# First mixer of a two-block network: the pooled half moved ahead of the heads and its projection between their halves

## What is computed

```python
def mixer_ab(x, norm, w_in, conv_w, conv_b, w_gx, b_gx, w_ga, b_ga, lam, w_pool, b_pool, pool_scale, w_out):
    z = rms_norm(x, norm) @ w_in
    z_gate = z[..., :W_A]
    z_rec = z[..., W_A:2 * W_A]
    z_pool = z[..., 2 * W_A:]
    xr = causal_dwconv(z_rec, conv_w, conv_b)
    y_a = jax.nn.gelu(z_gate) * rg_lru(xr, w_gx, b_gx, w_ga, b_ga, lam)
    y_b = multi_scale_pool(z_pool, w_pool, b_pool, pool_scale)
    return jnp.concatenate([y_a, y_b], axis=-1) @ w_out
```

## Time and profile before

| | |
|---|---|
| median of 3 runs | 3119.04 us (3116.56 to 3124.23) |
| the profiled execution | 3123.22 us |
| its span, first to last instruction | 3121.9 us |
| mean granted TensorE clock | 0.929 |

### The profile page before, as it was taken

How to read it: one execution, slowest core, us unless ns; L and a number is a source line. 1 busy time by engine, 2 the same in 40 slices (tenths; PEclk the granted TensorE clock), 3 DMA queues, 4 the chain that set the end, 5 groups by cost and what they waited for, 6 DMA issues and landing times. The chain is left out here.

```text
span 3121.9 us, 43004 instructions
## 1 busy us (share of the span) xinstructions
PE 2727.5 (87%) x18210; PEld 2154.1 (69%) x18210; DVE 1839.9 (59%) x2229; ACT 1216.8 (39%) x1553; POOL 279.5 (9%) x204
## 2 busy tenths in 40 slices
PE   6659999999999799999999798867869759399996
PEld 5437878888866378788887586645657647388885
DVE  5565545454568664454554665265565645399997
ACT  4434333232343342332323332233333212388884
POOL 1002000000000020100000100021120101123231
PEclk9879999999999899999999898979879889599998
DMA  4112322222211033222222342311110042499996
GB/s 149 51 45 92 121 81 95 95 95 95 101 60 49 23 106 107 81 95 95 95 95 95 108 155 98 121 34 24 24 32 15 6 152 85 185 374 378 383 369 235
DMA packets 88430, 366.74 MB, mean 117 GB/s; under 512 B 26032, under 2 KB 30256, under 8 KB 54320
## 3 DMA queue, kind: packets, MB, share of 16 engines
q1 hardware_dynamic: 78192, 339.33, 30.6%
q0 software_dynamic: 10048, 24.66, 2.3%
HBM read 346.62 MB, written 39.35 MB: 124 GB/s over the span
## 5 line engine op out<-in xcount | busy, mean ns | idle before, releaser
L471 PE MATMUL bank<-xg_hi,w_hi 128*128 128x512 f32 x1504 | 602.1, 400 | 11.9 <-DVE xg_lo L493 11.9
L471 PE MATMUL bank<-xg_lo,w_hi 128*128 128x512 f32 x1504 | 588.9, 392 | 0.0
L471 PE MATMUL bank<-xg_hi,w_lo 128*128 128x512 f32 x1504 | 588.8, 392 | 0.0
L458 DVE TENSOR_TENSOR w_lo<-w_raw,w_hi 128x2048 fp32r<-128x2048 f32 x165 | 378.0, 2292 | 218.3 <-ACT w_hi L454 217.9
L454 ACT ACTIVATE w_hi<-w_raw 128x2048 fp32r<-128x2048 f32 x165 | 314.2, 1905 | 275.6 <-PE bank L471 239.1
L471 PEld LDWEIGHTS bank<-xg_hi,w_hi 128*128 128x128 f32 x1504 | 285.3, 190 | 77.9 <-DVE w_lo L458 11.9
L471 PEld LDWEIGHTS bank<-xg_lo,w_hi 128*128 128x128 f32 x1504 | 285.0, 189 | 66.0 <-issue 7.5
L471 PEld LDWEIGHTS bank<-xg_hi,w_lo 128*128 128x128 f32 x1504 | 284.4, 189 | 60.2
L2771 DVE TENSOR_TENSOR w_lo<-e_w_raw,w_hi 128x2048 fp32r<-128x2048 f32 x77 | 174.5, 2285 | 11.2 <-ACT w_hi L2593 11.2
L2593 ACT ACTIVATE w_hi<-e_w_raw 128x2048 fp32r<-128x2048 f32 x77 | 147.7, 1918 | 29.9 <-PE bank L471 29.9
L609 DVE TENSOR_TENSOR x<-bank,x 128x512 f32<-128x512 f32 x88 | 60.5, 688 | 161.3 <-PE bank L471 161.3
(11 more groups left out here) (460 smaller groups left out, 5337.8 us busy)
## 6 DMA issues: line engine op xcount, KB each, us to landing
w_raw<-stream SPq DMA_DIRECT2D x165, 1024.0 KB, 4.9
e_w_raw<-expert_rows SPq DMA_DIRECT2D x63, 1024.0 KB, 9.6
w_raw<-expert_rows SPq DMA_DIRECT2D x33, 1024.0 KB
y_rows<-e_y_row SPq DMA_DIRECT2D x39, 512.0 KB
p_spill<-p_stage SPq DMA_DIRECT2D x36, 256.0 KB, 2.0
mix_gate<-p_spill SPq DMA_DIRECT2D x16, 256.0 KB, 4.6
na_bias<-bias_na SPq DMA_DIRECT2D x16, 224.0 KB, 4.6
rw_rkv<-p_spill SPq DMA_DIRECT2D x12, 256.0 KB, 6.4
```

The costliest lines, as they stand in the source:

```text
L458: V.tensor_tensor(ring(m)["lo"][m % SLOTS][:, :], ring(m)["raw"][m % RAW][:, :], ring(m)["hi"][m % SLOTS][:, :].bitcast(F32), ALU.subtract ...
L471: return T.matmul(out_ap, lhsT, rhs, start=first, stop=last, skip_group_check=True)
```

## The change

Five things change in the first mixer, and one at the start.

- The plan puts the pooled units first, then heads 0 to 4, then the two units of `ab_out_b`, then heads 5 to 7, then `ab_out_a`.
- A buffer `ab_under_y` lies in the same memory as `ab_y_hi` and `ab_y_lo`: the pooled groups' inputs and windows and all eight multipliers are kept there, each under the tile of y that is written later. The convolution's buffers are free all the time.
- TensorE projects the pooled groups first, does the group matmuls between heads 1, 2 and 3, and projects y's pooled half into tiles `xb` behind gates 3. Each other engine's order follows; ScalarE and VectorE run the first half's chain beside that, and VectorE adds the tiles `xb` to x between the outputs of heads 0 to 3.
- Behind the last gates TensorE opens six tiles `xa` with heads 0 to 3 (72 matmuls), and adds heads 4 to 7 when they are there.
- The norm tiles and the memory tiles now both run under `xa`, and GpSimd sums both in turns.
- At the start unit 1 is split before the squares and the reciprocal.

```diff
-    plan = [("ab_in", h) for h in range(8)] + [("pool_in", i) for i in range(2)]
-    plan += [("ab_out_a", i) for i in range(4)] + [("ab_out_b", i) for i in range(2)]
+    plan = [("pool_in", i) for i in range(2)] + [("ab_in", h) for h in range(5)]
+    plan += [("ab_out_b", i) for i in range(2)] + [("ab_in", h) for h in range(5, 8)]
+    plan += [("ab_out_a", i) for i in range(4)]
...
+        with ExitStack() as inner:
+            ab_under_y = sb(inner, "ab_under_y", [P, 2, KT, S])
...
+        act_split(A, 1)
...
+        dve_split(V, 1)
...
+    pool_u = [ab_under_y[:, 0, 4 + g, :] for g in range(4)]
+    pool_scratch = [[ab_under_y[:, 1, 4 + g, :], ab_tmp[g % 2][:, :]] for g in range(4)]
+    ab_mult = [ab_under_y[:, 1, h, :] for h in range(8)]
...
+        def open_out():
+            for j in range(ab_open):
+                n = units_of("ab_out_a", 4)[j // 2]
+                hi, lo = unit(n, 2 * P)
+                T.wait_ge(*w_lo.at(n))
+                cols = slice((j % 2) * P, (j % 2 + 1) * P)
+                b = take_bank(T, ("xa", j), dve_ab, "xa", j)
+                for k in range(4):
+                    T.wait_ge(*dve_ab.at("y_lo", k))
+                    split_matmul(T, b[:, :], hi[:, k, cols], lo[:, k, cols], ab_y_hi[:, k, :], ab_y_lo[:, k, :],
+                                 k == 0, False)
...
+        project_head(0)
+        project_head(1)
+        gates(0)
+        groups(0, 1)
+        project_head(2)
+        gates(1)
+        groups(2, 3)
+        project_head(3)
+        gates(2)
+        project_head(4)
+        gates(3)
+        pe_out(T, units_of("ab_out_b", 2), S, (ab_y_hi, ab_y_lo), range(4, 8), pe_ab, ("xb",),
+               ready=lambda k: dve_ab.at("yb_lo", k - 4))
+        project_head(5)
+        gates(4)
+        project_head(6)
+        gates(5)
+        project_head(7)
+        gates(6)
+        gates(7)
+        open_out()
+        pe_out(T, units_of("ab_out_a", 4), 2 * P, (ab_y_hi, ab_y_lo), range(KT), pe_ab, ("xa",), 1,
+               ready=lambda k: dve_ab.at("y_lo", k), opened={j: range(4, KT) for j in range(ab_open)},
+               after=lambda T: pe_xa_begin(T, 0))
...
-        for u in range(4):
-            pool_xa_mem(G, 0, u)
-        for i in range(1, 4):
+        pool_norm_sums(G, 1, lambda G, u: pool_xa_mem(G, 0, u))
+        for i in range(2, 4):
             pool_norm_sums(G, i)
```

More of the change, by code:

```diff
@@ L585, in pe_out, with act_out @@
             pe_norm_sums(T, i)
-    def act_out(A, units, cols, added, tag, i, xg_free, square_free, beside=None, after=None):
+    def act_out(A, units, cols, added, tag, i, xg_free, square_free, beside=None, after=None, taken=0):
         for u, n in enumerate(units):
-            act_take(A, n)
+            if u >= taken:
+                act_take(A, n)
             if beside:
@@ L598, in act_out, with dve_out @@
         act_norm_root(A, i)
-    def dve_out(V, units, cols, done, added, tag, i=None, bias=None, beside=None, after=None):
+    def dve_out(V, units, cols, done, added, tag, i=None, bias=None, beside=None, after=None, taken=0):
         for u, n in enumerate(units):
-            dve_take(V, n)
+            if u >= taken:
+                dve_take(V, n)
             if beside:
@@ new lines, in groups @@
+        def groups(*gs):
+            T.wait_ge(*group_load.at("w"))
+            for g in gs:
+                T.wait_ge(*dve_ab.at("pooled", g))
+                b = take_bank(T, ("group", g), dve_ab, "grouped", g)
+                matmul(T, b[:, :], ab_pool_w[:, g, :], pool_scratch[g][0]).then_inc(*pe_ab.mark("group", g))
+        def open_out():
[9 more added lines that the diff above has]
+                                 k == 0, False)
@@ L713, in pe_mixer @@
         for g in range(4):
             b = take_bank(T, ("pool", g), dve_ab, "u", g)
[L715 to L722, removed]
@@ L723, in pe_mixer @@
-        pe_out(T, units_of("ab_out_b", 2), S, (ab_y_hi, ab_y_lo), range(4), pe_ab, ("xb",), 1,
-               ready=lambda g: dve_ab.at("yb_lo", g), after=lambda T: pe_xa_begin(T, 0))
+            project(T, place[("pool_in", g // 2)], 2 * P, g % 2, ring1["xg"], range(KT), b, pe_ab, ("pool", g),
+                    xg_ready(0) if g == 0 else None)
+            if g == 2:
+                pe_start_sums(T)
+        project_head(0)
+        project_head(1)
+        gates(0)
+        groups(0, 1)
@@ L730, in act_mixer @@
     def act_mixer(A):
[L731 to L755, removed]
@@ L774, in act_mixer @@
[L774 to L785 removed]
+        head(0)
@@ new lines, in act_mixer @@
+        head(1)
+        gates(0)
+        head(2)
+        grouped(0, 1)
+        gates(1)
+        head(3)
+        grouped(2, 3)
+        gates(2)
+        head(4)
+        gates(3)
+        act_take(A, out_b[0])
+        multipliers(ab_halves[0])
+        act_take(A, out_b[1])
+        outputs(ab_halves[0])
+        head(5)
+        gates(4)
+        head(6)
+        gates(5)
+        head(7)
+        gates(6)
+        gates(7)
+        act_take(A, out_a[0])
+        multipliers(ab_halves[1])
@@ L787, in dve_decay @@
+        outputs(ab_halves[1])
+        act_out(A, out_a, 2 * P, dve_ab, ("xa",), 1, pe_ab.at("gate", KT - 1), None,
+                beside=lambda A, u: act_xa_mem(A, 0, u), after=lambda A: act_xa_begin(A, 0), taken=1)
     def dve_decay(V):
@@ new lines, in dve_mixer @@
+        head(0)
+        gate(0)
+        pool(0)
+        pool(1)
+        head(1)
+        gate(1)
+        gated(0)
+        pool(2)
+        pool(3)
+        head(2)
+        gate(2)
+        grouped(0, 1)
+        gated(1)
+        head(3)
+        gate(3)
+        grouped(2, 3)
+        gated(2)
+        head(4)
+        gated(3)
+        dve_take(V, out_b[0])
+        multipliers(ab_halves[0])
+        dve_take(V, out_b[1])
[3 more added lines that the diff above has]
+        add_b(2, 3)
@@ new lines, in dve_mixer @@
+        output(1)
+        add_b(4)
+        output(2)
+        add_b(5)
+        output(3)
+        add_b(6, 7)
+        head(5)
+        gate(5)
+        gated(4)
+        head(6)
+        gate(6)
+        gated(5)
+        head(7)
+        gate(7)
+        gated(6)
+        gated(7)
+        dve_take(V, out_a[0])
+        multipliers(ab_halves[1])
+        for h in ab_halves[1]:
+            output(h)
+        dve_out(V, out_a, 2 * P, pe_ab, dve_ab, ("xa",), 1, beside=lambda V, u: dve_xa_mem(V, 0, u),
+                after=lambda V: dve_xa_begin(V, 0), taken=1)
```

246 lines of the change are left out of this document (126 added, 120 removed).

## The result

| | before | after |
|---|---|---|
| median of 4 runs each, same chip | 3118.93 us | **3064.32 us** (3061.38 to 3066.81) |
| ratio after/before | | **0.9822** (0.9805 to 0.9839) |
| profiled execution; its span | 3123.22; 3121.9 | 3066.81; 3065.5 |
| mean granted TensorE clock | 0.929 | 0.936 |

The median is 54.6 us lower and 3.3 us above the forecast of 3061. It was the forecast case, inside the range.

A forecast was written before the change was run, and what follows sets the result against it. TensorE's standing still or lower clock was taken as the bound. The query tile moving from 320.4 to 262.1 saves 58.3 us: profiled 3123.22 becomes 3064.9, and the median, 4.2 lower, 3061; range 3042 to 3082.

The forecast's parts named there:

- Start: Start of the first mixer: pooled groups go first, head 0's weights come at 40.3, TensorE idles 2.0 us instead of 13.9.
- First heads: Heads 0 to 4 with gates and group matmuls: 64.5 us, to 104.8; VectorE's pooled work beside them costed at nothing.
- (c): Rival, first heads: pooled work not covered by heads 0 to 4, 21 us on VectorE in the open, 3082; chance 0.12.
- Pooled output: Projecting y's pooled half: tiles 0 to 3 to 116.0, 10.8 us idle for bank 2, tiles 4 to 7 to 140.0.
- (b): Rival, pooled output: bank 2 free in time or chain shorter, 3048; with the ping-pong at TensorE's pace, 3042; chance 0.10.
- Last heads: Heads 5 to 7 to 179.2; last tanh at 182.4, then 26.8 us until y is whole at 209.2.
- Output: Behind y: ScalarE and VectorE's ping-pong, first unit 2.0 + 4.4, three more of 10.0 each; last square at 244.7.
- Opened tiles: Six output tiles opened under the last heads' chain: 72 matmuls, 16.8 us, hidden; 13.2 of 30 us idle left.
- Behind the last square: End of the stage: the first query tile follows the last square by 17.4 us as before, at 262.1.
- (a): Rival, output stage: seven moved GpSimd memory adds stand fully in VectorE's way, 10.6 us, 3072; chance 0.10.
- (d): Rival, whole mixer: many short waits keep TensorE's clock low, up to 118 us slower, 3179; chance 0.03.
- (e): Rival: opened tiles or middle projection start late for a bank or weight, up to 16.8 + 22.4 back, 3100; chance 0.05.

The follow-up runs named there:

- tiles in pairs: Changed kernel, but in output tiles xa VectorE adds both banks of a unit to x before making the two norm tiles: 3062.11 us.
- spare bank: Changed kernel, but the bank that gate 4 holds is passed over before tile xb 4, one step more in the rotation: 3053.66 us.
- opening by head: Changed kernel, but heads 4 to 6 go to all six opened tiles as each becomes ready, leaving only head 7 for the output loop: 3062.89 us.
- short pooled output: Kernel with gate 4's bank passed over before tile xb 4, but only pooled group 0 projected, 72 of 96 matmuls left out: 3059.46 us.

## Why the prediction was right

**What bounds the kernel.** Confirmed. All of the gain but 3.7 us, no more than the scatter of the rest, lies ahead of the query tile, in TensorE's idle time (49.2 us) and clock (3.5). Predicted for the stage: 58.3; measured: 52.7. The total came within 3.3 us because the rest, which I had put at no change, gave 3.7, and that part is luck. With the rest unchanged the profiled execution would have taken 3070.5, 5.6 above the forecast of 3064.9 for it.

**Step by step**, my times against the trace:

| step | predicted | measured |
|---|---|---|
| head 0 starts, idle time before it | 40.3, 2.0 | 39.49, 2.2 |
| first heads end | 104.8 | 106.1 |
| first four pooled tiles end | 116.0 | 117.9 |
| wait for the bank, its end | 10.8, 126.8 | 11.1, 129.0 |
| last tanh starts | 182.4 | 185.05 |
| y whole | 209.2 | 211.87 |
| period of the output | 10.0 | 9.99 |
| last square done | 244.7 | 249.66 |
| query tile | 262.1 | 267.68 |

- *Start:* right. The reciprocal began at 33.94 and the split stood behind it, as set out.
- *First heads:* "I cost it at nothing" was right for the convolutions and wrong for one place. At 80.34 the matmul of group 3 waits 1.88 us: it needs the bank that group 0's result still fills, and VectorE reads it at 79.40, behind head 2's convolution and gate. So (c)'s mechanism exists, at 1.9 us and not 21 (1.7 in the tiles in pairs, 0.7 or 0.8 in the other experiments, where TensorE came there later).
- *Pooled output:* the wait of 10.8 was worked out, in no row, and measured 11.1. The chain ran as written: split on ScalarE at 118.00, square-root table at 119.92, `y_lo` 0 at 127.46, gate 4 at 128.26. The spare bank shows its cause. I was wrong to hold this wait for given ("only one bank is short" was the argument for (b)): one turn of a counter was enough, and 12.5 us were left lying.
- *Last heads:* from the last tanh to y 26.8 predicted, 26.8 measured.
- *Output:* the period was exact, the bound right: it is the ping-pong, as "tiles in pairs" shows. The term that was mis-sized is the first unit, "2.0 + 4.4". It took 2.3 more. Some 1.9 of that is VectorE's wait for the second tile: TensorE had worked in short pieces under the chain and came out of them at the lower clock:

```profile
211.90:217.77 5.87, 5.84 (x16) 4.63 (x17) 2.39 (x5) 2.76 (x6) 0.73 (x1) 0.61 0.15 47
217.77:226.00 8.23, 8.23 (x37) 6.59 (x36) 5.86 (x6) 4.47 (x7) 4.30 (x3) 1.00 0.14 27
```

  These are windows of the changed kernel: 16 matmuls in 5.9 us at 0.61, then 37 in 8.2 at 1.00. An estimate: at 0.233 each, the 15 matmuls from 211.93 to the end of the second tile would have been done at about 215.6, and VectorE would have come to it at 215.8 (213.61 + 2.2). By this the clock alone could make the wait, though the margin of 0.2 is thin and no run tests it by itself: opening by head removed the wait with fewer matmuls and the full clock at once. I had put 2 us for the clock on TensorE's own sum of 27.9, where it cost nothing, and none on the path that decides.
- *Opened tiles:* "16.8 us hide under this chain" was right, but their worth was never 16.8. It is 6.0, by the run without them, since the ping-pong covers the rest.
- *Behind the last square:* 17.4 predicted, 18.0 measured.

The differences add up: 2.7 up to y, 2.3 in the output, 0.6 behind it, 5.6 in all. The 2.7 are made up of 1.3 at the end of the first heads, 0.9 up to the end of the wait and 0.5 behind it, where the clock cost 2.6 us and the forecast had 2.

**The rule of the skill.** In the last stage a memory remainder takes 0.48 us while GpSimd is idle and 0.96 beside its adds, and an add takes 0.73 beside an addition to x, which reads a bank, and 1.51 in its pairs beside a split and a remainder. The Trainium skill (SBUF — State Buffer, "SBUF: two separate sides") says that VectorE's operations with two inputs in SBUF and GpSimd's exclude each other for whole instructions, and the trace agrees. What fell is my reading of it, that the adds stand "fully in VectorE's way": each remainder ran 0.48 longer, no more than what an add in progress can have left of its 0.73, and each add 0.78.

**The rivals.** (a) refuted, 3.5 us instead of 10.6, and those were in the forecast already; its sign, remainders of 0.96, came all the same and so could tell nothing. The row that I set against it was misread: in the trace before, each norm add began in the last 0.25 us of a remainder `xg_lo` (at 285.93, the remainder from 285.37 to 286.12). In the tiles in pairs a norm add was running when the second one began, and it took 1.32, not 0.75:

```profile
228.39 1.32 DVE L496 SCALAR_TENSOR_TENSOR xg_lo<-x,vec_sb,xg_hi 128x512 fp32r<-128x512 f32 x1 [0.39 <-ACT xg_hi L518]
```

(b) didn't happen; with the spare bank its first part does, at 3053.7, 10.7 below the changed kernel where I had priced 12.8. (c) by 1.9 us only. (d): the clock was 1.00 from 81 to 106 and from 141 to 179 us; it was 0.77 for 12 us behind the bank's wait, which the forecast had. (e): no unit or bank was late beyond the one named and that of group 3.

## What to carry to other kernels

An idle time that stands under a chain on other engines is best filled with work of another branch that is ready by then. Place the moved work on each engine's timeline with durations of the trace and follow every bank to its reader: a tile that lands in a bank which is read late turns a filled gap back into a wait, and skipping that bank may be all it takes. When the gap is filled, ask which hand-over between two engines now sets the pace. Here it was ScalarE and VectorE passing tiles one by one: a changed order of the same instructions brought 2.7 us, as much as moving more of TensorE's work under the chain (2.6), and only both together brought TensorE's first tiles and the new order to bear in every unit.

## What the runs showed of the hardware

- **A VectorE and a GpSimd operation delay each other one at a time.** GpSimd's first memory add, beside a VectorE operation that reads a bank and one buffer (the x add at 213.61), took 0.73 us; the pairs behind, beside VectorE's split and remainders, 3.02:

```profile
213.60 0.73 POOL L1061 TENSOR_TENSOR xa_sum<-xa_square 128x256 f32<-128x256 f32 x1 [185.31 <-ACT xa_square L1046]
...
222.33 3.02 POOL L1065 TENSOR_TENSOR xa_sum<-xa_sum,xa_square 128x256 f32<-128x256 f32 x2 [1.09 <-ACT xa_square L1046]
```

  GpSimd's operations doubled over VectorE's split of 2.29, yet the split itself, which had begun before them, stayed at 2.29, and the remainders behind it went from 0.48 to 0.96.
- **The lower clock costs where another engine waits for the first result behind a gap.** Behind 2.4 us of idle time and a short piece of work TensorE ran at 0.61, with matmuls 0.43 apart. The output as a whole had slack for that; its second tile had none, and by the estimate above that made VectorE's wait of 1.85 us.
- **Less work, lower clock.** With the pooled output cut, TensorE stood still for 13.2 us in the place of the 72 matmuls left out (16.8 us), and its granted clock from 121 to 136 us was 0.75, against 1.00 where they kept it busy. Windows of the short pooled output, then of the spare bank alone:

```profile
121.00:136.00 15.00, 11.23 (x35) 8.52 (x36) 12.37 (x17) 5.55 (x9) 0.00 (x0) 0.75 0.24 79
```

```profile
121.00:136.00 15.00, 14.48 (x63) 11.46 (x62) 12.53 (x16) 7.93 (x12) 0.00 (x0) 1.00 0.23 80
```
